# Hybrid GLA and short-convolution trunk on eight cores: narrow matmuls spread among wide groups, second norm ended in the next tile, GLA steps seven groups apart

## What is computed

```python
h = rmsnorm(x, norm1_g[l])
proj = jnp.einsum('bsd,de->bse', h, w_in[l])
q, k, v, r, fz, gb_in, gc_in, cx, ga, gb = jnp.split(proj, split_pts, axis=-1)
fg = jnp.einsum('bsr,rk->bsk', fz, w_fg2[l]) + b_fg[l]     # fz has 16 columns
log_a = jax.nn.log_sigmoid(fg) / GATE_TAU
o = gla_chunk_causal(qh, kh, vh, ah)      # chunks of 64, 4 heads, state 128x256
o = o * lax.rsqrt(jnp.mean(o * o, axis=-1, keepdims=True) + NORM_EPS) * gla_norm_g[l]
y_a = jnp.einsum('bsv,vd->bsd', o.reshape(b_sz, s_len, VAL_WIDTH) * jax.nn.silu(r), w_oa[l])
conv = causal_depthwise_conv(gc_in * cx, conv_w[l], conv_b[l])      # width 3
y_b = jnp.einsum('bsc,cd->bsd', gb_in * conv, w_ob[l])
mix = jax.nn.sigmoid(ga) * y_a + jax.nn.sigmoid(gb) * y_b
x = x + jnp.einsum('bsd,de->bse', mix, w_o[l])
h2 = rmsnorm(x, norm2_g[l])
hid = jax.nn.silu(h2 @ w_ffn_gate[l]) * (h2 @ w_ffn_up[l])      # 2816 wide
x = x + jnp.einsum('bsf,fd->bsd', hid, w_ffn_down[l])
```

## Time and profile before

| what | value |
|---|---|
| median of 3 runs | 5062.94 us (the lowest 5062.35) |
| profiled execution | 5063.73 us |
| its span, first to last instruction, slowest core | 5062.7 us |
| spans of the eight cores | 5041.4 to 5062.7 us |
| TensorE busy | 4811.1 us, 95% |
| VectorE busy | 2086.6 us, 41% |
| ScalarE busy | 2218.1 us, 44% |
| memory traffic of the core | 208 GB/s over the span |
| share of the chain that ended last | PE 81%, ACT 6%, DMA 4%, DVE 4% |

### The profile page before, as it was taken

One profiled execution on the slowest core, in us unless ns is written; L12 is line 12 of the kernel. 1 busy time (PEld: TensorE's weight loads), 2 busy tenths in 40 slices (PEclk: granted clock), 3 DMA queues, 4 the chain that ended last, 5 costly groups with the idle time before them and its releaser, 6 DMA issues.

```text
span 5062.7 us, 66511 instructions; the slowest of 8 cores (5041.4 to 5062.7 us)
## 1 busy us (share of the span) xinstructions
PE 4811.1 (95%) x22464; PEld 2165.7 (43%) x22464; DVE 2086.6 (41%) x3486; ACT 2218.1 (44%) x4481; POOL 189.8 (4%) x362
## 2 busy tenths in 40 slices
PE   6999999999999999999899999999999999999998
PEld 2444444444444444444344444434444444444443
DVE  2544353433535345253252534435344353443633
ACT  3454353544535444353343544435344354543533
POOL 0000000000000000000000000000000000000000
PEclk9999999999999999999899999999999999999999
DMA  6768989786553444444567888877755444343343
GB/s 136 136 130 153 193 158 207 180 201 185 168 183 127 138 158 142 154 140 139 126 134 172 146 163 176 174 190 181 190 192 165 159 140 148 140 150 137 134 153 116
DMA packets 131197, 798.91 MB, mean 158 GB/s; under 512 B 13074, under 2 KB 13330, under 8 KB 66612
## 3 DMA queue, kind: packets, MB, share of 16 engines
q0 software_dynamic: 51552, 336.81, 34.3%
q1 hardware_dynamic: 78866, 457.64, 26.2%
q10 hardware_dynamic: 450, 0.22, 0.0%
HBM read 936.24 MB, written 114.36 MB: 208 GB/s over the span
## 4 chain that ended last, share of the span: by engine, by line
PE 81%; ACT 6%; DMA 4%; DVE 4%; issue 3%; ACTq 0%; DVEq 0%; POOL 0%; SPq 0%; POOLq 0%
PE pb L278 75%; ACT sb_sg L302 2%; ACT sb_sg L300 2%; DMA scr<-sb_wsl 2%; DVE sb_h L329 1%; PE pb L404 1%; DMA sb_wsl<-w 1%; PE pb L317 1%; PE pb L444 1%; PE pb L393 1%; ACT sb_sg L304 1%; DVE sb_xT L329 1%; DMA sb_xT<-x 1%; PE pb L380 1%; ACT sb_sqj L482 1%
## 5 line engine op out<-in xcount | busy, mean ns | idle before, releaser
L278 PE MATMUL pb<-sb_h,sb_wsl 128*128 128x512 bf16 (+1 forms) x11392 | 2630.3, 384 | 86.5 <-DVE sb_dgm L307 32.5
L278 PEld LDWEIGHTS pb<-sb_h,sb_wsl 128*128 128x128 bf16 (+1 forms) x11392 | 1103.8, 99 | 1478.7 <-issue 242.7
L307 DVE TENSOR_TENSOR sb_sg<-pb,sb_sg 128x512 f32<-128x512 f32 x608 | 418.2, 691 | 1485.2 <-ACT sb_sg L304 1012.3
L300 ACT ACTIVATE sb_sg<-pb 128x512 f32<-128x512 f32 x736 | 434.4, 590 | 1178.5 <-PE pb L278 1178.3
L278 PE MATMUL pb<-sb_hid,sb_wsl 128*128 128x512 bf16 x2816 | 631.4, 380 | 9.7 <-DMA sb_wsl<-w 7.5
L278 PE MATMUL pb<-sb_wsl,sb_h 128*128 128x512 bf16 x2560 | 621.2, 392 | 5.3 <-DVE sb_sg L307 3.5
L302 ACT ACTIVATE sb_sg<-sb_sg 128x512 f32<-128x512 f32 x736 | 464.1, 631 | 69.8 <-ACT sb_sg L300 3.0
L304 ACT ACTIVATE sb_sg<-sb_sg 128x512 f32<-128x512 f32 x736 | 464.0, 630 | 68.8 <-ACT sb_sg L302 1.8
L278 PEld LDWEIGHTS pb<-sb_hid,sb_wsl 128*128 128x128 bf16 x2816 | 275.4, 98 | 344.3 <-issue 19.1
L278 PEld LDWEIGHTS pb<-sb_wsl,sb_h 128*128 128x128 bf16 x2560 | 253.5, 101 | 355.4 <-issue 93.3
L313 ACT ACTIVATE sb_sq<-sb_xT 128x512 bf16<-128x512 f32 x320 | 195.9, 623 | 403.7 <-DVE sb_xT L604 322.3
(11 more groups left out here) (58 smaller groups left out, 2404.5 us busy)
## 6 DMA issues: line engine op xcount, KB each, us to landing
sb_wsl<-scr SPq DMA_DIRECT2D x248, 1024.0 KB, 5.1
sb_wsl<-w POOLq DMA_DIRECT2D x168, 1024.0 KB, 10.4
sb_wsl<-scr SPq DMA_DIRECT2D x76, 768.0 KB, 4.9
sb_wsl<-scr SPq DMA_DIRECT2D x80, 704.0 KB, 4.2
scr<-sb_wsl POOLq DMA_DIRECT2D x52, 1024.0 KB, 13.6
sb_wsl<-w POOLq DMA_DIRECT2D x52, 768.0 KB, 8.4
sb_wsl<-w POOLq DMA_DIRECT2D x48, 704.0 KB, 8.7
sb_xT<-x SPq DMA_DIRECT2D x8, 2048.0 KB, 20.8
```

Of the source, the lines that this page charges most:

```text
L278: ins = P.matmul(out, a, b, start=(j == 0), stop=(j == n - 1))
L300: k = act.do(A.activation(out=buf[:], in_=pb[b][:, :], func=AF.Exp, scale=-1.0))
L307: return V.tensor_tensor(out=out, in0=a, in1=b, op=ALU.mult)
```

## The change

The unit list and the way it is merged are changed, with a few of the engines that read out banks.

- The eight 16-column matmuls of the gate code no longer form a group. `u_fzq(hh)` makes one query group with one 16-column matmul behind its fourth and one behind its eighth wide matmul; the gate code keeps a bank over the four. Each wide matmul of a query waits for its own chunk of `h1` only. ScalarE reads out the gate code, behind the last query.
- `u_fg` comes behind the second to fifth value group, `u_cum` behind the fifth to eighth, and `u_gam(ts)` is four matmuls for one sub-tile, behind the sixth to eighth value group and the first key group.
- The first two value groups of the first half are read out by ScalarE, the other two by VectorE (they alternated).
- The GLA steps stand 7 groups apart: `g_U` at 7 ts and 7 ts + 2, `g_C` at 7 ts + 5, `g_T` at 7 ts + 10, so that `g_T(3)` is behind the last group of `rest`, ahead of the gates.
- `u_n2` is handed to the next tile and placed behind its second query group; in the last tile it stays.
- `woven` knows a `sep`: a unit with it is taken only when so much feed-forward cost has been done since the last mixer unit. The first `u_o` has 22, one down projection, and `u_n2` of the last tile too. `lead` is 72, not 40, `tail` 66 for the last mixer list.
- `wfg` holds both layers and is loaded once at the start. The float32 identity lies in a sigmoid buffer.

```diff
-        t_id = load(act, ident32[:], cst_d[:, 0:128], "c_id")
+        t_id = load(act, sgb[0][:, 0:128], cst_d[:, 0:128], "c_id")
...
-        wfg_sem = newsem("c_wfg")
-        nc.scalar.dma_start(out=wfg[0:17, :], in_=wfg_d[0]).then_inc(wfg_sem, 16)
-        t_wfg = (wfg_sem, 16)
+        t_wfg = load(act, wfg[0:17, :, :], wfg_d.rearrange("l r c -> r l c"), "c_wfg")
...
-        t_id16 = dve.do(V.tensor_copy(out=ident16[:], in_=ident32[:]))
+        t_id16 = dve.do(V.tensor_copy(out=ident16[:], in_=sgb[0][:, 0:128]))
+        sg.free[0] = (sgb[0], t_id16)
...
-                    if l > 0:
-                        sp.after(st["fza_used"])
-                        nc.sync.dma_start(out=wfg[0:17, :], in_=wfg_d[l]).then_inc(wfg_sem, 16)
-                    loc["wfg"] = (wfg_sem, 16 * (l + 1))
...
-            def u_fz():
-                u_begin()
...
+            def u_fzq(hh):
+                if hh == 0:
+                    u_begin()
...
-                pe.after(*st["h1"])
-                b, k = fm(w, 0, h1r, 16)
-                dve.after(k, st["fza_used"], t_fza1)
-                loc["fza"] = dve.do(V.tensor_copy(out=fza[0:16, :], in_=pb[b][0:16, :]))
-                banks.give(b, loc["fza"])
-            add(8, "fzq", u_fz)
...
-            def u_q(hh):
-                b, k = fm(W(i, "fzq"), 16 + hh * 128, h1r)
+                if hh == 0:
+                    loc["zb"], fr = banks.take()
+                    pe.after(fr)
+                zb = loc["zb"]
+                b, fr = banks.take()
+                pe.after(fr)
+                for kc in range(KC):
+                    pe.after(st["h1"][kc])
+                    ins = P.matmul(pb[b][:, :], w[:, kc, 16 + hh * 128:144 + hh * 128], h1r(kc), start=(kc == 0), stop=(kc == KC - 1))
+                    if kc == KC - 1:
+                        k = pe.do(ins)
+                    if kc % 4 == 3:
+                        z = hh * 2 + kc // 4
+                        ins = P.matmul(pb[zb][0:16, :], w[:, z, 0:16], h1r(z), start=(z == 0), stop=(z == KC - 1))
+                        if z == KC - 1:
+                            kz = pe.do(ins)
...
-            for hh in range(4):
-                add(8, "fzq", lambda hh=hh: u_q(hh))
+                if hh == 3:
+                    act.after(kz, st["fza_used"], t_fza1)
+                    loc["fza"] = act.do(A.activation(out=fza[0:16, :], in_=pb[zb][0:16, :], func=AF.Copy))
+                    banks.give(zb, loc["fza"])
...
             def u_fg(ts):
...
-                pe.after(fr, loc["fza"], (wfg_sem, 16 * (l + 1)))
-                k = pe.do(P.matmul(pb[b][:, :], fza[0:17, ts * 128:(ts + 1) * 128], wfg[0:17, :], start=True, stop=True))
+                pe.after(fr, loc["fza"], t_wfg)
+                k = pe.do(P.matmul(pb[b][:, :], fza[0:17, ts * 128:(ts + 1) * 128], wfg[0:17, l, :], start=True, stop=True))
...
-            def u_gam():
+            def u_gam(ts):
...
-                pe.after(fr, *loc["spb"])
-                for ts in range(NTS):
-                    for hh in range(4):
-                        c = ts * 8 + hh * 2
-                        ins = P.matmul(pb[b][:, c:c + 2], spb_v[:, ts, hh * 128:(hh + 1) * 128], msk[:, 128:130], start=True, stop=True)
+                pe.after(fr, loc["spb"][ts])
+                for hh in range(4):
+                    ins = P.matmul(pb[b][:, hh * 2:hh * 2 + 2], spb_v[:, ts, hh * 128:(hh + 1) * 128], msk[:, 128:130], start=True, stop=True)
...
-                loc["gam"] = act.do(A.activation(out=gam[:, :], in_=pb[b][:, 0:32], func=AF.Exp))
-                banks.give(b, loc["gam"])
+                loc["gam"][ts] = act.do(A.activation(out=gam[:, ts * 8:(ts + 1) * 8], in_=pb[b][:, 0:8], func=AF.Exp))
+                banks.give(b, loc["gam"][ts])
...
             def u_v(hf, ts):
...
-                if ts % 2:
+                if (ts < 2) if hf == 0 else (ts % 2):
...
-            for ts in range(NTS):
-                add(2, None, lambda ts=ts: u_fg(ts))
+            for hh in range(4):
+                add(10, "fzq", lambda hh=hh: u_fzq(hh))
+                if hh == 1:
+                    us.extend(late)
...
-                if n < 4:
-                    add(2, None, lambda n=n: u_cum(n))
-                if n == 4:
-                    add(9, None, u_gam)
+                if 1 <= n < 5:
+                    add(2, None, lambda n=n: u_fg(n - 1))
+                if n >= 4:
+                    add(2, None, lambda n=n: u_cum(n - 4))
+                if n >= 5:
+                    add(4, None, lambda n=n: u_gam(n - 5))
...
+                if ts == 0:
+                    add(4, None, lambda: u_gam(3))
...
-                gla[ts * 8] = [(2, lambda ts=ts: g_U(ts, 0))]
-                gla[ts * 8 + 2] = [(2, lambda ts=ts: g_U(ts, 1))]
-                gla[ts * 8 + 5] = [(4, lambda ts=ts: g_C(ts))]
-                if ts < 3:
-                    gla[ts * 8 + 9] = [(3, lambda ts=ts: g_T(ts))]
+                gla[ts * 7] = [(2, lambda ts=ts: g_U(ts, 0))]
+                gla[ts * 7 + 2] = [(2, lambda ts=ts: g_U(ts, 1))]
+                gla[ts * 7 + 5] = [(4, lambda ts=ts: g_C(ts))]
+                gla[ts * 7 + 10] = [(3, lambda ts=ts: g_T(ts))]
...
-                if dc == 0:
-                    add(3, None, lambda: g_T(3))
...
-                add(9, "o%d" % (dc // 4), lambda dc=dc: u_o(dc))
-            add(1, None, u_n2)
-            return us
+                add(9, "o%d" % (dc // 4), lambda dc=dc: u_o(dc), 0 if dc else 22)
+            return us, [Unit(1, None, u_n2, 22 if i == NL - 1 else 0)]
...
         def norm1_end(i, k):
...
-            out, cm, cf = [], 0, 0
+            out, cm, cf, ahead = [], 0, 0, 0
...
-                if m and (not f or cf >= due):
+                if m and (not f or (cf >= due and cf >= ahead + m[0].sep)):
...
+                    ahead = cf
...
-        order = []
-        for i in range(NL + 1):
-            m = mix_units(i) if i < NL else []
-            f = ffn_units(i - 1) if i > 0 else []
-            order += woven(m, f, 40, 22)
...
+        order, late = [], []
+        for i in range(NL):
+            m, late = mix_units(i, late)
+            if i == NL - 1:
+                m += late
+            order += woven(m, ffn_units(i - 1) if i > 0 else [], 72, 66 if i == NL - 1 else 22)
+        order += ffn_units(NL - 1)
```

17 lines of the change are left out of this document (8 added, 9 removed).

## The result

The changed kernel takes 4905.91 and 4907.24 us (the second is the profiled execution, span 4906.2), the kernel before 5062.35 and 5062.94. The ratio is 0.969, interval 0.965 to 0.973: faster. By the profiled executions 156.5 us went (5063.7 − 4907.2), where 151 were forecast. In some executions of every version the cores of one die or both show a lower granted clock and the time is longer, which is why the median over all four of the changed kernel is 5121.73 us; the others are compared here, and in two experiments cores 0 to 3 alone.

The account below looks back on a forecast made before the run. TensorE, busy 95% of the span, was taken as the bound, losing time to waits and slow-clock matmuls behind them; gains of 192.7 us less costs of 35.5 and 6 gave 151, so 5063.7 to 4913 us, range 4880 to 4975.

Parts of the forecast that it names:

- part 7: Second norm's last sum, moved behind the second query group: TensorE's waits on its late square go, gain 15.2 us.
- 1, the last transpose: g_T(3) moved to the end of the conv groups: idle time and slow matmuls behind it go, gain 52.3 us.
- 2, the decay matmuls: Decay matmuls in four pieces between wide groups: clock stays up, slow wide matmuls behind go, gain 31.1 us.
- 3, the gate matmuls: Gate matmuls one at a time among wide ones: slow matmuls behind bunches and a bank wait go, gain 24.8 us.
- 4, the gate code's bank: Gate code read out last by ScalarE: its bank wait goes, gain 21.7 us, and 0.5 of slow matmuls.
- 5, the gate weights: Both layers' gate weights loaded at the start: the second layer's wait and slow matmuls behind go, gain 21.7 us.
- 6, the first output group: A down projection ahead of the first output group covers the last merge's wait, gain 14.9 us.
- 8 and 9, the ends: Last tile: down projections kept for the last norm, 7.1 us; start: first query waits for h1 by chunk, 3.4 us.
- (a): Dips behind narrow float32 work stay though it is spread: 4966 us; chance 0.15, with part of (b) or without.
- (b): Gain given back to waits for converted weights and a doubled GLA stretch: 4955 us; chance 0.15.
- (c): Sprinkled narrow matmuls pull the clock down through the query and first value stretch: 5215 us, slower; chance 0.04.
- (d): Dips and GLA waits go altogether and crossings cost nothing: 4851 us; chance 0.11 for it or part of it.

Follow-up runs that it names:

- part 1 alone: Kernel before, with only the GLA steps seven groups apart and the last transpose ahead of the gates: 5025.1 us at the lowest, ratio 0.992.
- the first experiment: Changed kernel with the last transpose g_T(3) put back behind the first two gate groups: 4925.29 us.

## Why the prediction came out right in sum, and where its terms were off

The forecast was 151 us, the profiled executions give 156.5. The mechanism is borne out: the waits of parts 1 to 6 and the slow matmuls behind them went. The step that failed outright is part 7: it gave the late square of the earlier trace rows to the second norm and took 15.2 us for moving that norm's end. The square is the final norm's, the row of waits fell by 4.7 us, and the move is worth 0 to 2 us in the time. Next to it the price of cutting the decay matmuls had the wrong sign (4.8 us of cost, 9 us of gain), and the 8.3 us for single gate matmuls and 8.5 us of new slow groups in the r stretch were missed. These errors cancel, so that the sum is nearer than its terms; that is luck. One by one:

**1, the last transpose (52.3).** The wait and the slow matmuls behind it are gone, and in the old order they were worth what was said: 53 by the trace of part 1 alone, of which 34 to 38 arrive in the time. In the new order the position is worth only 18, since the new merge would have shortened that wait anyway. The term's reading, that u_oa has no matmul ahead of it, was true but not the whole: 2.4 of the 3.73 us (3.73 less the 1.35 of the first experiment) were VectorE standing behind a sigmoid.

**2, the decay matmuls (31.1).** Right: 31.5 behind them went, +34 when they are bunched again, −36 to −40 alone. The cost (4.8) had the wrong sign. The pieces take 51.8 us (0.101 for each of 512 passes), the bunches 60.8 (0.119): 9 us cheaper. I had priced the entries and not asked whether the bunch itself ran at the full rate. It did in three tiles, at 3.49 us (0.109 a pass); the others take 3.58 to 4.31. So 5 of the 9 us are the bunch's own time at the low clock, and 4 are left for the shape.

**3, the gate matmuls (24.8).** Right, 21.6 behind and the bank waits are gone; but the cost of 8.3 isn't there. They take 67.5 us before and 67.4 after, start to next start. A bunch of three is 0.31 cheaper than three single ones, but in the second layer one bunch took 5.41 us where others take 2.84, and two single ones 1.97 and 2.01 where others take 1.05, which gave the saving back. No run has this part by itself.

**4, the gate code's bank (22.2).** Right as a wait; alone it gives 35 to 38.

**5, the gate weights (21.7).** Right as a wait (19.8 + 1.8, which is 21.6); alone it gives 32. Here and in 4 the edit gives 10 us and more beyond its own place. The timelines show 9 us (here) and 6 us (in 4) less of slow groups behind gate, decay and transpose matmuls that the edit did not touch, and in 4 also 6 us less for the gate and decay matmuls themselves. Why the dips elsewhere become fewer is open.

**6, the first output group (14.9).** Right: the wait fell from 16.3 to 1.4, and 13.1 of it come back without the down projection. The 20 us of that run hold 8.8 more of excess in the r stretch, where the kernel before had none behind sb_dgm, so they are no part of the gain over it.

**7, the second norm's last sum (15.2).** Wrong, the step that failed. The waits on squares fell, without the start, from 23.1 to 18.4 us, and putting the step back costs 0 to 2 us. I took the earlier trace rows for the second norm's last square. The engines around it in the kernel before show whose it is:

```profile
4610.12 0.59 PE L317 MATMUL pb<-sb_sq,sb_ones 128*128 128x512 bf16 x2
...
4610.60 0.69 ACT L324 ACTIVATE sb_rstd<-pb,sb_epsb 128x512 f32<-128x512 f32 x1 [3.40 <-PE pb L317]
...
4611.92 0.61 ACT L313 ACTIVATE sb_sq<-sb_xT 128x512 bf16<-128x512 f32 x1
```

Two sums come at 4610.12. The second norm's root begins at 4610.60, so its last sum is one of them and waited for nothing. Behind the root ScalarE does one more square at 4611.92, of the final norm, which layer two also sums behind its last down projection, and the matmul at 4612.67 waits for that. In the changed kernel ScalarE has no root in between, the square comes right after VectorE's addition, and the wait is still there, 1.51 us:

```profile
4467.65 0.69 DVE L723 TENSOR_TENSOR sb_xT<-pb,sb_xT 128x512 f32<-128x512 f32 x1 [3.83 <-PE pb L279]
4468.49 0.63 ACT L314 ACTIVATE sb_sq<-sb_xT 128x512 bf16<-128x512 f32 x1 [4.03 <-DVE sb_xT L723]
4469.26 0.38 PE L318 MATMUL pb<-sb_sq,sb_ones 128*128 128x512 bf16 x1 [1.51 <-ACT sb_sq L314]
```

**8 and 9, the ends (7.1 and 3.4).** The wait in the last tile is gone (sb_h 12.0 to 2.7 holds both). The start gave 1.2: the first matmul starts at 48.75 where it started at 49.93. The wait there fell by 4.6 us, but x landed 3.5 us later.

**Costs.** The crossings: 0.20 us a pair, as forecast; the eight single matmuls and their entries take 22 us more than one group by the timeline, 17 by the run. The r and GLA stretch: +9.5 where 6 were taken, within its bounds.

**The clock.** The mean clock gave back 102 us and 76 were claimed. By the list of slow wide groups 88.0 us went down to 19.8: those behind the named places (78 by this list) are gone, and 8.5 came new behind the waits of the r stretch. The rest of the 102 I put down to the clock in waits and in narrow work, where it is not time won one for one; that is by elimination. As a check the mean was looser than I took it.

**The account.** All rows of the table of waits sum to 235.8 us before and 138.9 after, 97 less; slow wide groups 68 less; decay matmuls 9 less; norm sums and transposes 5 less; crossings 22 and cumulative decay 2 more: 155 of the 156.5. The sum of 151 was as near as it was because part 7 (too high by 10 to 14), the start (by 2), the r stretch (by 3) and the new slow groups there (8.5, not foreseen) were outweighed by the decay pieces (too low by 14), the gates (by 8) and the 5 us of norm sums and transposes.

**The rivals.** (a) fell: not one slow group behind narrow float32 work in pieces, and a clock of 0.995. (b) did not come: weights are waited for 17.6 us in the two rows, 21.5 before. (c) fell: query groups show 0.97 for four wide ones and the way in. (d) was half right, the dips went, the waits of the r stretch and the crossings stayed. A middle tile takes 298 us (the groups ahead of the wait for sb_dgm start at 1229.87 and 1527.67), as forecast.

## What to carry to other kernels

On an engine that is the bound, read what stands behind a wait or a run of narrow matmuls, not only the wait: here the wide matmuls behind waits of 2 to 4 us cost more than half of the wait again (19.9 us on 33.5), behind waits of 1.4 us nothing, and behind a bunch of tiny float32 matmuls they cost with no wait at all, until the bunch was cut into pieces of 0.8 us. Before a wait is given to a step, look at all engines around the row, down to which instance of the repeated line it is; two norms share a line here, and the term that rested on the wrong one was worth next to nothing. And narrow matmuls of another column count are cheapest in one group: only those that pull the clock down are worth spreading.
